# Large experts of a mixture of experts take 96 rows in two packings of the array instead of 128 rows in one

## The reference, cut to what matters

```
g    = argmax(softmax(t @ wg + bg))             # 1 of 4 groups
v, i = top_k(softmax(le of group g), 2)         # 2 of its 4 experts
comb[token, expert] = p_group * v / sum(v)      # 0 for experts not chosen
hid  = silu(t @ w_gate[e]) * (t @ w_up[e]) * comb[:, e]     # 1024 -> 512, 16 experts
out  = sum over e of hid @ w_down[e]                        # 512 -> 1024
x    = layer_norm(ALPHA * x + g2 * out)
```

## Time and profile before

| | |
|---|---|
| median of 3 runs | 485.66 us (484.97 to 485.97) |
| the profiled execution | 484.4 us, span 482.6 us |
| mean granted TensorE clock | 0.971 |
| PE busy | 435.2 us (90% of the span) |
| DVE, ACT busy | 247.7 us, 121.0 us |
| DMA | 149.48 MB, mean 310 GB/s |
| expert loop | 216.2 us to about 462 us |

### The profile page before, as it was taken

How to read it: one execution, slowest core, us unless ns; L and a number is a source line. 1 busy time by engine, 2 the same in 40 slices (tenths; PEclk the granted TensorE clock), 3 DMA queues, 4 the chain that set the end, 5 groups by cost and what they waited for, 6 DMA issues and landing times.

```text
span 482.6 us, 6404 instructions
## 1 busy us (share of the span) xinstructions
PE 435.2 (90%) x2352; PEld 230.7 (48%) x2352; DVE 247.7 (51%) x462; ACT 121.0 (25%) x229; POOL 39.9 (8%) x41
## 2 busy tenths in 40 slices
PE   0789999999999987799999999999999999899850
PEld 0434555555444452694554355555555544355220
DVE  4462725747873787980223343335544455333766
ACT  3300185384301033251120111111111111121143
POOL 2000042054000001560000000000000000000000
PEclk9989999999999997899999999999999999999995
DMA  8999994308999883627999999999999999999303
GB/s 310 387 387 375 296 387 155 140 0 208 387 393 404 316 322 135 231 62 264 333 396 396 348 363 389 396 389 393 396 394 390 393 396 394 390 393 402 143 2 131
DMA packets 65364, 149.48 MB, mean 310 GB/s; under 512 B 3625, under 2 KB 4505, under 8 KB 64937
## 3 DMA queue, kind: packets, MB, share of 16 engines
q1 hardware_dynamic: 63776, 143.33, 80.6%
q10 hardware_dynamic: 1384, 5.46, 2.9%
q0 software_dynamic: 160, 0.10, 0.4%
HBM read 147.28 MB, written 1.60 MB: 309 GB/s over the span
## 4 chain that ended last, share of the span: by engine, by line
PE 76%; DMA 8%; DVE 5%; issue 5%; ACT 4%; SPq 1%; DVEq 0%; ACTq 0%
PE PS L1721 18%; PE PS L1518 13%; PE PS L1600 9%; PE PS L1761 8%; PE PS L1727 6%; PE PS L1795 4%; DMA ring<-in_w_in 4%; DMA ring<-in_ex_w_gate 4%; PE PS L1456 3%; PE PS L1682 3%; PE PS L1501 2%; PE PS L1768 1%; PE PS L1803 1%; PE PS L1741 1%; PE PS L1835 1%
## 5 line engine op out<-in xcount | busy, mean ns | idle before, releaser
L1721 PE MATMUL PS<-ring,xs 128*64 128x256 f32 x896 | 102.9, 382 | 1.2 <-DMA ring<-in_ex_w_gate 1.2
L1721 PEld LDWEIGHTS PS<-ring,xs 128*64 128x64 f32 x896 | 61.9, 137 | 37.6 <-issue 9.1
L1518 PE MATMUL PS<-hT,ring 128*128 128x388 f32 x192 | 67.0, 501 | 2.9 <-DMA ring<-in_w_in 2.1
L1761 PE MATMUL PS<-ring,hTs 128*64 128x512 f32 x224 | 51.2, 598 | 2.1 <-ACT hTs L680 1.3
L1518 PEld LDWEIGHTS PS<-hT,ring 128*128 128x128 f32 x192 | 36.8, 194 | 31.3 <-issue 3.6
L1265 DVE SCALAR_TENSOR_TENSOR y<-PS,comb,y 128x1024 f32<-128x1024 f32 x39 | 49.8, 1277 | 0.3 <-PE PS L1803 0.3
L1761 PEld LDWEIGHTS PS<-ring,hTs 128*64 128x64 f32 x224 | 14.8, 136 | 30.9 <-issue 30.7
L1251 DVE TENSOR_TENSOR yl<-PS,yh 128x512 fp32r<-128x512 f32 x12 | 8.3, 692 | 41.3 <-ACT yh L698 41.3
L1727 PE MATMUL PS<-ring,xs 128*128 128x512 f32 x64 | 28.0, 592 | 0.0
L698 ACT CAST yh<-PS 128x512 fp32r<-128x512 f32 x12 | 7.0, 586 | 81.3 <-PE PS L1761 62.8
L1195 DVE SCALAR_TENSOR_TENSOR hid<-sg,PS 128x256 f32<-128x256 f32 x14 | 5.9, 421 | 39.4 <-PE PS L1721 39.4
(11 more groups left out here) (269 smaller groups left out, 551.2 us busy)
## 6 DMA issues: line engine op xcount, KB each, us to landing
ring<-in_ex_w_gate SPq DMA_DIRECT2D x16, 2048.0 KB, 13.1
ring<-in_ex_w_up SPq DMA_DIRECT2D x16, 2048.0 KB, 13.5
ring<-in_ex_w_down SPq DMA_DIRECT2D x16, 2048.0 KB, 13.9
ring<-in_w_ada SPq DMA_DIRECT2D x12, 2048.0 KB, 15.9
ring<-in_w_in SPq DMA_DIRECT2D x3, 2048.0 KB, 20.6
ring<-in_w_out SPq DMA_DIRECT2D x2, 2048.0 KB, 17.8
rows<-row_scratch ACTq DMA_DIRECT2D x3, 1024.0 KB, 7.6
xn<-in_x_sample SPq DMA_DIRECT2D x2, 512.0 KB, 6.5
```

The source lines that it names most:

```text
L1518: mm = pe.matmul(PS[:, w % 4, 0:W], wt[:, k, (w % 4) * P:(w % 4 + 1) * P], hT[:, k, :], start=(k == 0), stop=(k == KD - 1))
L1721: mm = pe.matmul(PS[HALF * h:HALF * (h + 1), j, 0:FE // 2], x[:, k, 0:HALF], w[:, k, h * (FE // 2):(h + 1) * (FE // 2)], start=(k == 0), s ...
L1761: mm = pe.matmul(PS[HALF * h:HALF * (h + 1), yb, :], x, w[:, f, h * 512:(h + 1) * 512], start=(f == 0), stop=(f == KF - 1))
```

## The change

`CAP` goes from 128 to 96. The `many` form of each step no longer uses the full array. It takes rows 0 to 63 as `few` does, on two column tiles of 64, and then rows 64 to 95 on four column tiles of 32: each tile takes the same 32 rows and a quarter of the output columns. The hidden rows of the second part lie in columns 256 to 383 of `sg` and `hid`, four blocks of 32 partitions, one for each quarter. `hTs` needs three transposes instead of four. The output of the second part lies in 256 columns of bank `yb + 1`; a constant mask of ones and zeros (`C_PAR`) moves it into two parts of `yh` and `yl` whose rows of the wrong quarter are zero. `choose` builds a second selection matrix `selR` for these rows, and `combine` multiplies both.

The core of the diff:

```diff
-CAP = P
-PASSES = TOK // CAP
+CAP = 3 * P // 4
+REST = CAP - HALF
+PASSES = 1 + -(-(TOK - CAP) // P)
@@ project_in, many
-                        mm = pe.matmul(PS[:, j, :], x[:, k, :], w[:, k, :], start=(k == 0), stop=(k == KD - 1))
+                        for h in range(2):
+                            pe.matmul(PS[HALF * h:HALF * (h + 1), j, 0:FE // 2], x[:, k, 0:HALF],
+                                      w[:, k, h * (FE // 2):(h + 1) * (FE // 2)], start=(k == 0), stop=(k == KD - 1))
+                    for k in range(KD):
+                        for q in range(KF):
+                            mm = pe.matmul(PS[REST * q:REST * (q + 1), j, FE // 2:MF], x[:, k, HALF:CAP],
+                                           w[:, k, P * q:P * (q + 1)], start=(k == 0), stop=(k == KD - 1))
@@ turn
-                fork(pe, counts[e], lambda: tiles(2), lambda: tiles(4))
+                fork(pe, counts[e], lambda: tiles(2), lambda: tiles(3))
@@ project_out, many
+                        x = hTs[:, f % 2, HALF * (f // 2):HALF * (f // 2 + 1)]
                         for h in range(2):
-                            mm = pe.matmul(PS[:, yb + h, :], hTs[:, f, :], w[:, f, h * 512:(h + 1) * 512],
-                                           start=(f == 0), stop=(f == KF - 1))
+                            pe.matmul(PS[HALF * h:HALF * (h + 1), yb, :], x, w[:, f, h * 512:(h + 1) * 512],
+                                      start=(f == 0), stop=(f == KF - 1))
+                    for f in range(KF):
+                        for q in range(KF):
+                            mm = pe.matmul(PS[REST * q:REST * (q + 1), yb + 1, 0:256], hTs[:, 2, REST * f:REST * (f + 1)],
+                                           w[:, f, 256 * q:256 * (q + 1)], start=(f == 0), stop=(f == KF - 1))
@@ combine, many
+                    for r in range(2):
+                        rows_, to = (selR[:, e % 2, :], slice(512, 1024)) if r else (m, slice(0, 512))
+                        for q, part in enumerate(parts):
+                            for h in range(2):
+                                mm = pe.matmul(PS[:, b + h, :], rows_[HALF * h:HALF * (h + 1), i * P:(i + 1) * P],
+                                               part[HALF * h:HALF * (h + 1), to], start=(first and (r, q) == (0, 0)),
+                                               stop=(stop and (r, q) == (1, 1)))
@@ choose, both forms
+                    if e >= LAST - 1:
+                        dve.nop().then_inc(s["wrem"], 4)
+                    dve.nop().then_inc(s["selB"], 2)
+                    first_rows()
...
+                    dve.tensor_scalar(seltmp[:, :], Prow[:, 0, :], io[:, 1, e:e + 1], None, ALU.is_equal)\
+                        .then_inc(s["selB"], 1)
+                    dve.wait_ge(s["selB"], 2 * e + 1)
+                    dve.scalar_tensor_tensor(out=selR[:, e % 2, :], in0=Prow[:, 1, :], scalar=io[:, 1, e:e + 1],
+                                             in1=seltmp[:, :], op0=ALU.is_equal, op1=ALU.add).then_inc(s["selB"], 1)
@@ y_out and y_low, many: the second half in two parts of 256 columns, scaled by the mask
+                    for q in range(2):
+                        last = act.activation(dst[:, 512 + 256 * q:768 + 256 * q], PS[:, yb + 1, 0:256], ACT.Copy,
+                                              scale=scales[q])
```

More of the change, by code:

```diff
@@ L86, in constants @@
     c[:, C_ROW] = np.arange(P) % HALF
-    for pb in range(PASSES):
-        c[:, C_ROW + 1 + pb] = np.arange(P) + pb * CAP
+    c[:, C_ROW + 1] = HALF + np.arange(P) % REST
+    for pb in range(1, PASSES):
+        c[:, C_ROW + 1 + pb] = np.arange(P) + CAP + (pb - 1) * P
+    for q in range(2):
+        c[:, C_PAR + q] = np.arange(P) // REST % 2 == q
     c[:, C_SEG:C_SEG + 3 * NE] = (np.arange(3 * NE) % NE != 0)
@@ L151, in build @@
         cond32 = keep("cond32", [P, KD, 38])
+        selR = at("selR", mrow0, [P, 2, TOK], F32R)
+        assert mrow0 + 2 * TOK * 4 <= place[0]
         cmod = keep("cmod", [P, 2, KD, 2])
@@ L355, in overflow @@
                 with eng.Fori(1, PASSES) as pb:
-                    with eng.If(most > pb * CAP):
+                    with eng.If(most > pb * P - (P - CAP)):
                         with eng.Fori(0, NE) as e:
@@ L1151, in _ @@
             for pb in range(PASSES):
-                step(dve.tensor_scalar(cnt[:, 1 + NE + pb * NE:1 + NE + (pb + 1) * NE], off, float(pb * CAP),
+                step(dve.tensor_scalar(cnt[:, 1 + NE + pb * NE:1 + NE + (pb + 1) * NE], off,
+                                       float(CAP + (pb - 1) * P if pb else 0),
                                        float(NSLOT), ALU.add, ALU.min))
@@ L1211, in choose, with weight_sum @@
                     dve.wait_ge(s["wrow_sb"], 2)
-                def weights_of(q):
+                def weight_sum(q, name, before):
                     for c in range(2):
@@ new lines, in many @@
+                def many():
+                    if e >= LAST - 1:
+                        n = 4 * (e - LAST + 1)
+                        weight_sum(1, "wrem", n)
+                        for q in range(2):
+                            dve.scalar_tensor_tensor(out=wl[:, e % 2, 1 + q:2 + q], in0=wacc[:, 0:1], scalar=wacc[:, 1:2],
+                                                     in1=cst[:, C_PAR + q:C_PAR + q + 1], op0=ALU.add, op1=ALU.mult)\
+                                .then_inc(s["wrem"], 1)
+                        dve.wait_ge(s["wrem"], n + 4)
+                    dve.tensor_scalar(seltmp[:, :], Prow[:, 0, :], io[:, 1, e:e + 1], None, ALU.is_equal)\
[3 more added lines that the diff above has]
+                                             in1=seltmp[:, :], op0=ALU.is_equal, op1=ALU.add).then_inc(s["selB"], 1)
+                    dve.wait_ge(s["selB"], 2 * e + 2)
+                    first_rows()
@@ L1235, in y_low @@
+                fork(dve, counts[e], few, many)
             def y_low(e):
@@ L1800, in many @@
                 def many():
-                    for q, part in enumerate(parts):
-                        for h in range(2):
-                            mm = pe.matmul(PS[:, b + h, :], m[:, i * P:(i + 1) * P], part[:, h * 512:(h + 1) * 512],
-                                           start=(first and q == 0), stop=(stop and q == 1))
+                    for r in range(2):
[5 more added lines that the diff above has]
+                                               stop=(stop and (r, q) == (1, 1)))
                     mm.then_inc(done, 1)
```

98 lines of the change are left out of this document (54 added, 44 removed).

## The result

| kernel | median us (lowest to highest, runs) | ratio to before (95%) |
|---|---|---|
| before, beside it | 485.82 (484.97 to 486.05, 4) | |
| changed | 541.06 (538.36 to 543.3, 4) | 1.1148 (1.111 to 1.1187) |

The changed kernel is 11.5% slower. The forecast was 482.0 us and 73% for faster; it is wrong by 59 us, in sign and in size. The profiled execution took 538.36 us, with a span of 536.6 us (before: 484.4 and 482.6), so 54.0 us are to be found between two traces.

A forecast was written before the change was run, and what follows sets the result against it. Weights at 394 GB/s were taken to set the end, through early DMA gaps behind large experts' PE steps. Gaps closed 5.4 us, less 1.6 for program text and 0.1 for nops, gave 3.7 us: 485.66 to 482.0 us, range 480.0 to 485.2.

The forecast's parts named there:

- What bounds the kernel: Expert loop: weights at 394 GB/s set the end, through early DMA queue gaps while SP waits for large experts' PE steps.
- The new steps: Large experts on PE: gate or up 6.87 to 5.4 us, down 7.06 to 5.4 us, combine 1.1 to 1.3 us.
- two abreast: Rival, 5%: four tiles of 32 run only two at once, second part 3.6 us, kernel slower at 489 us.
- The start: Path into the expert loop: the added `cnt` row delays it by 0.11 us.
- The gaps: DMA queue at 220 to 225, 230 to 235 and 270 to 285 us: closing gains 1.4 + 1.7 + 2.3 = 5.4 us.
- The number of packets: Queue q8: near 55 instruction packets in all instead of 29, with forms that are jumped over fetched as well.
- What a packet costs: DMA queue in the loop: 23 more packets at 1.08 us on one of 16 engines cost 1.6 us.
- The rival of the program stalls: Rival, 11%: PE waits for its own program in the loop, 49 s - 9.2 us for a stall s per packet; slower.
- Text eats the gain: Rival, 12%: packets cost 3.1 us and four tiles the upper price, leaving 0.4 us gain, 485.3 us.
- all of it arrives: Rival, 3%: all of PE's 9.2 us saved in the large experts' steps reach the end, 476.5 us.

The follow-up runs named there:

- experiment 6: Changed kernel, but new PE forms for experts 0 and 3 alone and GpSimd's `xn` steps started after `route_done`: 482.12 us, ratio 0.9944 to the kernel before.
- experiment 2: Kernel before, with the new forms of gate, up and down added as never-run text for the 14 small experts: 529.61 us, ratio 1.0899.
- experiment 9: Changed kernel and kernel before, each loading one eighth of the columns from the eighth weight matrix on: 488.67 us changed, 484.88 us before.
- experiment 3: Kernel before with the never-run new forms for 14 experts, their text jumped over in two hops instead of one: 533.1 us, ratio 1.0989.

## Why the prediction was wrong, point by point

- **What bounds the kernel: right.** PE and the weights both, with gaps of the DMA queue in front of the large experts' steps. Closing them moved the end (experiment 6).
- **The new steps: right.** Gate and up 5.49 us (forecast 5.4), down 3.58 + 1.86 = 5.44 (5.4), combine 1.12 (1.1 to 1.3). Four tiles of 32 do run four abreast: 1.89 us for 64 records, so the rival "two abreast" (3.6 us) is out.
- **The start: wrong.** "Less 0.11 us for the added row of `cnt`" was 2.3 us plus 1.6 us behind it, at a lower clock. The row that it was priced by the earlier trace rows stood right behind one of 2.32 us for an operation of the same size, which the prediction left out.
- **The gaps: right in place, somewhat too large in size.** 5.4 us forecast; 3.5 us closed and 2.7 us gained once the start is the same for both.
- **The number of packets: right.** Near 55 forecast, 54 found. That forms which are jumped over are fetched was right as well (50 packets in experiment 2).
- **What a packet costs: the step that failed.** "23 more packets cost 1.6 us" prices them as load on the DMA engines. They cost PE its instructions. I took the 1.08 us that a packet moves for the time in which it can be had, and held it against the 3.60 us between two crossings. From the start of the branch to its end it took up to 5.3 us: up to 2.9 us until the packet moved, 1.1 us of transfer and 1.4 us until it ran. With light loads in the queue the 55 us of long branches are 10.5 (experiment 9). "Against it: the 19 now left no hole" argued from packets 11 us apart on average; they were to come at 2.2 times that rate.
- **The rival of the program stalls: the right mechanism at 11%, with one sum too small.** Its line, 49 s - 9.2 us, gives 32 us with the 40.9 / 48 = 0.85 us a packet that were found. It lacked what a hole brings behind it, 16.5 us and more of steps at half the clock, and the late start. Its rule of the Trainium skill (Runtime: NRT & Kernel Launch, "Instruction fetch mechanics"), a stall where a taken branch leaves the window that has been fetched, I had used against the rival, since no jump passes a whole packet. Experiment 3 shows that shorter jumps do not help, and the hole at 393.62 and nine others stand inside a block. The trace agrees with the stall itself and shows 55 us of it; the same section calls a plain crossing mostly hidden, and that held here only with few packets (before) or an empty queue (experiment 9).
- **Text eats the gain, all of it arrives: out.** PE waited for no expert weights at all in the changed kernel, so the queue had slack.

What stays open: why the packet for a given crossing comes in time or not. The traces show when a packet is moved, not when it is asked for. The kernels differ in how much text a small expert has and in where the crossings fall, and these two were not varied apart.

## What to carry to other kernels

Count the program as a stream that must arrive: packets of an engine's text per unit of work, the forms that are jumped over included, against the time between two packets while weights fill the DMA engines (5.7 us or more here). A second form for the rare case is cheap if what both forms share stands once ahead of the fork (487.9 instead of 541.1 us here), or if it stands only where it is used. And a step that is added to a short chain is priced by what runs beside it on GpSimd, not by its neighbour's duration.

## What the runs showed that was not expected

- A 128 x 16 cast on DVE takes 0.17 us alone and 2.32 us beside a GpSimd step of 2.4 us on 128 x 1024 numbers, and ends with it, before and after.
- A hole of 2.2 us in PE's work is followed by steps of 5.35 us instead of 3.6 (granted clock 0.72 in the window), a hole of 3.3 us by a window at 0.72 and one at 0.86. Not each hole does it: after the 2.29 us at 276.61 the next step took 3.65 us.
- Text that never runs cost some 44 us of 485 (experiment 2).
- Half of PE's holes, 20.3 of 40.9 us, are at no branch: straight text waits for its packet too.
